# The last eight modulation slabs of a two-block transformer kernel move into the output half of x's first feed-forward

## The chip, the cores and the metric

The kernel runs on one core of a Trainium2 chip. The metric is the time of one execution on the device in microseconds (us), and the median over several runs is what is compared. The five engines of the core are called as in the profile: PE (TensorE), DVE (VectorE), ACT (ScalarE), POOL (GpSimd) and SP (SyncE, which here only issues transfers).

## The reference

Two blocks run one after the other on 256 tokens of width 1024. The first block is attention with a token selection, a short convolution and a layer of 16384 one-neuron experts, of which each token picks 128. The second block takes the first one's output x and a context of 256 tokens. Each block's norms, gates and shifts are modulated by columns that come out of one matrix product with a condition vector:

```python
mod_x = (jax.nn.silu(c) @ w_ada[l] + b_ada[l])[:, None, :]
mod_c = (jax.nn.silu(c_ctx) @ w_ada[l] + b_ada[l])[None, None, :]
sh1x, sc1x, g1x, sh2x, sc2x, g2x, sh3x, sc3x, g3x = jnp.split(mod_x, N_MOD, axis=-1)

x = x + 0.5 * g1x * swiglu(modulate(rmsnorm(x, norm_ffn1[l]), sh1x, sc1x), w13_ffn1[l], w2_ffn1[l])
ctx = ctx + 0.5 * g1c * swiglu(modulate(rmsnorm(ctx, norm_ffn1[l]), sh1c, sc1c), w13_ffn1[l], w2_ffn1[l])
qc, kc, vc, gc, fc, gac, gfc = project(modulate(rmsnorm(ctx, norm_mix[l]), sh2c, sc2c), w_in[l])
...
x = x + g2x * y_x
x = x + 0.5 * g3x * swiglu(modulate(rmsnorm(x, norm_ffn2[l]), sh3x, sc3x), w13_ffn2[l], w2_ffn2[l])
return rmsnorm(x, norm_final)
```

The second block's w_ada is 1024 by 9216: 18 slabs of 512 columns. The first ten hold shift 1, scale 1, gate 1, shift 2 and scale 2; the last eight hold gate 2, shift 3, scale 3 and gate 3, which are wanted only for x, from the mixer's residual on. The context needs nothing of them.

## The kernel before

All weights stream from device memory through one buffer, `ring`, in slabs of 128 partitions by 4096 words (2048 KB; the slabs of a feed-forward's output matrix w2 have 2816 words, 1408 KB). SP issues the slabs in one fixed list (`slab_order`), each as soon as PE has released the slab that held its slot. Up to the experts and the context the ring has four slots. From x's first feed-forward on (`second_at`) it has three (`SPLIT_RING`), and the fourth holds the rounded copies described below.

A modulation slab is used in `mod_steps`. Slab m gives a row group on PE (eight matmuls of the condition columns with the slab), ACT copies the row to `mod_row`, PE turns it into columns (four matmuls of two columns, in `mod_turn`), and ACT copies these to `mod1` or `mod2`. The turn of slab m-1 stands behind the row group of slab m; the last one of a list has its own turn at the end. There are 30 slabs: 0 to 11 for the first block, 12 to 29 for the second.

The program in order of time, as far as it matters here:

- The head: the first block's projections, attention and out projection, with modulation slabs 0 to 14 between them; then the expert queries; then `mod_steps(15, 30)`, fifteen slabs with nothing between them. Beside that, DVE chooses the experts of the first 128 tokens (`choose_experts(0)`).
- The expert loop: 128 batches of two gathered rows each. POOL issues a gather of 1024 KB (128 rows of 8 KB) into one of eight buffers, DVE takes a dot product with it (L1587), ACT applies gelu, DVE scales and sums (L1598), PE sums the other row of the batch. Before its first dot product DVE waits for the last modulation slab: `v.wait_ge(*emptied("mod29"))`. The context's feed-forward and projections are dealt out in pieces between the batches, at fixed batch numbers.
- x's first feed-forward, tag `f1`: eleven slabs of w13, then eight slabs of w2, whose results are called `f1_y0` to `f1_y7`. These products are done in three matmuls of rounded parts. So each slab is cut into pieces (four, or three for w2); ACT writes the upper part of a piece (L924), DVE the rest (L1231), and PE waits for the piece. Four pieces can be ahead.
- The norm `x2`, then the projections `gf`, `f` and so on to the end.

What ACT does during `f1_y` is written out in `norm_hi`: for k from 0 to 7 it calls `ahead("f1_y<k>")`, waits until DVE has added the result to x, and squares block k of x. `ahead(name)` makes an engine first split every piece up to three behind the last piece of `name`. DVE calls the same `ahead` ahead of each of its additions (`take`, L1333). Both engines run their instructions strictly in the order written.

```python
def ahead(name):
    q = piece_of[name]
    split_until(min(q + PIECES, phase_end(q)) - 1)
```

Of the kernel before, what the change touches and what calls it, by code (L numbers as in the profile page):

```python
# [14 lines left out]
P = 128  # L15
# [23 lines left out]
KF = FF // P  # L39
FG = 4  # L40
MODS = [("w_ada", i) for i in range(12)] + [("w_ada_2", i) for i in range(18)]
RING = 4
SLAB = 4096
SPLIT_RING = 3
# [63 lines left out]
def slab_order():  # L108

    mods = [(name, i, SLAB) for name, i in MODS]  # L110
    ffn = lambda n: [(f"w13_ffn{n}", i, SLAB) for i in range(11)] + [(f"w2_ffn{n}", i, KF * P) for i in range(8)]
    w_in_2 = {"q": (0, 2), "k": (2, 4), "v": (4, 8), "g": (8, 12), "f": (12, 14), "ga": (14, 16), "gf": (16, 18)}
    proj = lambda n: [("w_in_2", i, SLAB) for i in range(*w_in_2[n])]
    w_in = lambda i: [("w_in", i, SLAB)]
    out_proj = [("w_out", i, SLAB) for i in range(2)]
    peer = lambda i: [("peer_wq", i, SLAB)]
    first = (mods[:4] + w_in(0) + [("w_idx", 0, KD * 136)] + w_in(1) + w_in(2) + w_in(4) + w_in(5) + w_in(6) + w_in(3)
             + mods[4:13] + out_proj + mods[13:15] + peer(0) + peer(1) + peer(2) + peer(3) + mods[15:])
    context = ffn(1) + proj("k") + proj("v")
    second = (ffn(1) + proj("gf") + proj("f") + [("p_four", i, SLAB) for i in range(2)] + proj("ga") + proj("q")  # L120
              + proj("k") + proj("v") + proj("g") + [("p_ret", i, SLAB) for i in range(4)]
              + [("w_out_2", i, SLAB) for i in range(2)] + ffn(2))
    return first + context + second, len(first) + len(context)
# [33 lines left out]
def program(nc, dram, out):  # L157
# [2 lines left out]

    slabs, second_at = slab_order()
    slots, last_in_split = slots_of(slabs, second_at)
    split = [n for n in range(len(slabs)) if n >= second_at or slabs[n][0] in ("w_in", "w_out", "peer_wq")]
    pieces = [(n,) + cut for n in split for cut in cuts(*slabs[n][:2])]
    first_out = sum(slabs[p[0]][0] == "w_in" for p in pieces)
    first_pieces = sum(p[0] < second_at for p in pieces)
    with ExitStack() as ctx:
        def sb(name, width, dt=F32):
            return ctx.enter_context(nc.sbuf_tensor(name, [P, width], dt))
# [33 lines left out]
        found = sb("found", 2 * PH * PSEL, U32)  # L203
        place = sb("place", SLOTS, U32)
        spare = sb("spare", 2 * PSEL, U32)

        def param(name):
            at, w = PARAM_AT[name]
            return prm[:, at:at + w]
# [42 lines left out]
        probs = [arena[:, G0 + 7936:G0 + 8960].rearrange("p (h s) -> p h s", h=HEADS),  # L252
                 arena[:, F0 + 3072:F0 + 5120].rearrange("p (h s) -> p h s", h=HEADS)]
        subkeys = arena[:, G0 + 9984:G0 + 12032].rearrange("p (h n) -> p h n", h=2 * PH)
        mod_row = small[:, 1536:2560].rearrange("p (a n) -> p a n", a=2)
        y_att = arena[:, F0 + 5120:F0 + 6144].rearrange("p (j t) -> p j t", j=KA)

        pq_t = arena[:, G0:G0 + 4096].rearrange("p (h t) -> p h t", h=2 * PH)
# [106 lines left out]
        def _(pe):  # L365
# [29 lines left out]
            def mm(o, a, b, first, last):  # L395
                return nc.tensor.matmul(o, a, b, start=first, stop=last)  # L396
# [11 lines left out]
            def mod_turn(m):  # L408

                pe.wait_ge(*emptied(f"row{m}"))  # L410
                o = begin(f"mod{m}", "act")
                a, w = (0, 1) if MODS[m][0] == "w_ada" else (1, 2)
                for j in range(4):
                    last = mm(o[:, j * w:(j + 1) * w], mod_row[:, m % 2, j * P:(j + 1) * P], const("pick3")[:, a:a + w], True, True)
                end(last)
                turned[0] += 1

# [90 lines left out]
            def split_feed_forward(tag, m, f):  # L508
                need = norm_need(m)
                for i in range(11):  # L510
                    for half, who in ((0, "act"), (1, "dve")):
                        name = f"{tag}_{'ab'[half]}{i}"
                        o = begin(name, who)
                        for j in range(2):
                            _, w_hi, w_lo = next_piece()
                            for k in range(KD):
                                if k in need:
                                    pe.wait_ge(*need.pop(k))
                                last = three(o[:, j * L:(j + 1) * L], w_hi[:, k, :], w_lo[:, k, :], h_hi[:, k, :],
                                             h_lo[:, k, :], k == 0, k == KD - 1)  # L520
                            piece_end(last, name if j else None)
                for i in range(8):
                    o = begin(f"{tag}_y{i}", "dve")
                    for part in range(3):
                        (k0, k1, _, _), w_hi, w_lo = next_piece()
                        if i == 0:

                            pe.wait_ge(sem("hid_split"), 11 * f + k1 // 2)
                        for k in range(k0, k1):
                            last = three(o[:, 0:L], w_hi[:, k - k0, :], w_lo[:, k - k0, :], hid_hi[:, k, :],  # L530
                                         hid_lo[:, k, :], k == 0, k == KF - 1)
                        piece_end(last, f"{tag}_y{i}" if part == 2 else None)

            def squares_by_block(tag, sq=sq2):
                o = begin("ss_" + tag, "dve")
# [105 lines left out]
            for t in range(NT):  # L641
                for i in range(2):
# [1 line left out]
                    for j in range(4):  # L644
                        last = nc.tensor.transpose(o[:, j * P:(j + 1) * P], h_t[:, 4 * i + j, t * P:(t + 1) * P], ident)
                    end(last)
            mod_steps(15, 30)
            at = [0]

            def ctx_end(name, ins):  # L650
# [251 lines left out]
        def _(act):  # L902
# [58 lines left out]
            def mod_row_of(m):  # L961
                if m >= 2:

                    act.wait_ge(group_done, index[f"mod{m - 2}"] + 1)
                copy_out(f"row{m}", mod_row[:, m % 2, :])

            def mod_turned(m):
                turned[0] += 1
# [15 lines left out]
            def norm_hi(tag, m, shift, names, sq=sq2, hi=h_hi):  # L984

                for k in range(KD):
                    if names:
                        name = names[k * len(names) // KD]
                        ahead(name)
                        act.wait_ge(*emptied(name))  # L990
                    nc.scalar.activation(sq[:, k, :], x_t[:, k, :], ACT.Square).then_inc(sem("sq_" + tag), 1)
                root(rstd[:])
                if m is not None:
                    normed_hi(m, shift, hi)
# [94 lines left out]
            for t in range(NT):  # L1089
                for i in range(2):  # L1090
                    copy_out(f"ht{t}_{i}", h2[:, t, i * BANK:(i + 1) * BANK])
            mod_steps(15, 30)

            def context():

# [117 lines left out]
        def _(v):  # L1213
# [331 lines left out]
            def context():  # L1545
# [1 line left out]
                yield 0  # L1547
                step(TT(mod1[:, 40:48], mod1[:, 40:48], param("b_ada")[:, 40:48], ALU.add))
                m2 = mod2[:].rearrange("p (j s) -> p j s", s=2)
                step(TT(m2, m2, param("b_ada_2").unsqueeze(2).to_broadcast([P, 72, 2]), ALU.add))  # L1550
                for key, row, s in (("ctx1", 2, 1), ("x1", 2, 0), ("x3", 8, 0)):
                    step(TS(half_gate[key], mod2_v[:, row, :, s], 0.5, None, ALU.mult))
                yield done_at["ss_ctx1"] + 1
                v.wait_ge(sem("ctx_landed"), 16)
# [21 lines left out]
            v.wait_ge(*emptied("ks1_3"))  # L1576
            v.sem_inc(sem("row_free_pe"), GBUF // 2)
            v.sem_inc(sem("row_free_dve"), GBUF // 2 + 1)
            v.wait_ge(*emptied("mod29"))

            def dot_batch(n):

# [63 lines left out]
            v.wait_ge(sem("late"), 64)  # L1646
            split_ff_dve("f1", 0, half_gate["x1"])
            split_modulated("x2", 3, param("norm_mix_2"), mod2_v[:, 4, :, 0], mod2_v[:, 3, :, 0])
            ahead("f3")
            for i in range(4):  # L1650
                o = take(f"mx{i}")
# [166 lines left out]
```

## Time and profile before

| | |
|---|---|
| three runs, median (lowest to highest) | 2064.69 us (2057.81 to 2064.85) |
| the profiled execution, its own time | 2061.91 us |
| its span in the trace | 2060.1 us |
| granted PE clock, mean of the span | 0.915 of full |
| PE busy | 1746.9 us, 85% |
| DVE busy | 1265.4 us, 61% |
| ACT busy | 601.0 us, 29% |
| POOL busy | 433.6 us, 21% |
| moved from device memory | 535.86 MB, 261 GB/s over the span |

Busy shares are means over stages with different limits. The trace gives for each instruction its start from the span's beginning, its length, the idle time of its engine before it and what ended that idle time. For a transfer it gives the time from issue to landing. The profiled execution's own time exceeds its span by 1.8 us, which lies outside of the program.

### The profile page before, as it was taken

The numbers are of one execution on the slowest core, as the hardware profiler recorded it, in microseconds if no ns is written. First come the engines' busy times: TensorE is split into PE (matmuls) and PEld (weight loads), VectorE is DVE, ScalarE is ACT, GpSimd is POOL, SyncE is SP. The second block draws the span as 40 slices with busy tenths as digits, with TensorE's granted clock in tenths as the row PEclk, the third lists the DMA queues.
The fourth block names the chain that finished last, engine by engine and source line by source line (L and its number), as shares of the span: only waits on it lengthen the run. The fifth ranks groups of instructions, "written<-read, shape, count | busy, mean of one in ns | idle before, by whom it ended". The sixth has DMA issues, their size and how long they took to land.

```text
span 2060.1 us, 25356 instructions
## 1 busy us (share of the span) xinstructions
PE 1746.9 (85%) x9904; PEld 1349.1 (65%) x9904; DVE 1265.4 (61%) x2226; ACT 601.0 (29%) x899; POOL 433.6 (21%) x344
## 2 busy tenths in 40 slices
PE   5996898668787877866689669999999999999997
PEld 2984794335554545543333227999879996689997
DVE  2674366288788786766867575564525645665554
ACT  3434342211111110000000016754434443245442
POOL 1550461033333334333334310000000000000000
PEclk7998798689998998888899779999999999999999
DMA  7446638989999999999899961445425452153542
GB/s 327 154 186 273 262 128 376 426 359 387 397 353 381 367 389 379 387 406 387 350 411 403 403 248 69 178 166 189 158 82 202 170 202 82 47 199 130 198 147 100
DMA packets 57570, 538.51 MB, mean 261 GB/s; under 512 B 6384, under 2 KB 6512, under 8 KB 7152
## 3 DMA queue, kind: packets, MB, share of 16 engines
q1 hardware_dynamic: 20592, 268.48, 33.4%
q0 software_dynamic: 36864, 268.45, 32.7%
q8 instruction: 78, 1.28, 0.3%
q14 instruction: 36, 0.29, 0.0%
HBM read 535.86 MB, written 1.05 MB: 261 GB/s over the span
## 4 chain that ended last, share of the span: by engine, by line
PE 60%; DMA 22%; DVE 8%; issue 6%; POOL 2%; ACT 1%; POOLq 0%; DVEq 0%; another core or an unknown queue 0%; SPq 0%; ACTq 0%
PE psum L396 60%; DMA arena<-in_experts,idx_stage 17%; DMA ring<-in_w_ada 3%; POOL arena L895 1%; DVE arena L1598 1%; DMA ring<-in_w_in 1%; DVE rstd L1258 1%; DVE small L1597 1%; DVE small L1595 0%; DVE arena L1587 0%; DVE h_t L1292 0%; ACT upper L924 0%; DVE small L1587 0%; DVE h_t L1272 0%; DVE h_t L1270 0%
## 5 line engine op out<-in xcount | busy, mean ns | idle before, releaser
L396 PE MATMUL psum<-arena,small 128*128 128x512 f32 x560 | 322.2, 708 | 204.2 <-DVE small L1597 204.0
L1587 DVE CUSTOM_DVE_ANT_0 arena<-arena 128x1024 f32<-128x1024 f32 x256 | 313.7, 1225 | 239.3 <-DMA arena<-in_experts,idx_stage 179.4
L1231 DVE TENSOR_TENSOR ring_r<-ring,ring_r 128x1024 fp32r<-128x1024 f32 (+1 forms) x240 | 287.7, 1207 | 277.1 <-ACT ring_r L924 276.0
L396 PE MATMUL psum<-small_r,ring_r 128*128 128x256 f32 x2304 | 417.0, 281 | 9.4 <-DVE h_t_r L1298 9.4
L895 POOL DMA_INDIRECT arena<-in_experts,idx_stage x256 | 297.5, 1162 | 410.1 <-PE psum L396 333.8
L396 PEld LDWEIGHTS psum<-small_r,ring_r 128*128 128x128 f32 x2304 | 361.8, 189 | 11.2 <-issue 10.5
L396 PEld LDWEIGHTS psum<-arena,small 128*128 128x128 f32 x560 | 114.3, 216 | 356.2 <-DVE small L1597 250.6
L396 PE MATMUL psum<-h_t_r,ring_r 128*128 128x256 f32 x1152 | 329.9, 286 | 0.0
L396 PE MATMUL psum<-arena_r,ring_r 128*128 128x256 f32 x2208 | 326.3, 281 | 2.8 <-DVE arena_r L1280 2.8
L924 ACT ACTIVATE ring_r<-ring 128x1024 fp32r<-128x1024 f32 (+1 forms) x240 | 248.7, 1042 | 217.0 <-PE psum L396 213.8
L396 PEld LDWEIGHTS psum<-arena_r,ring_r 128*128 128x128 f32 x2208 | 290.6, 189 | 3.3 <-DVE arena_r L1280 3.2
L1133 ACT ACTIVATE small<-small 128x2 f32<-128x2 f32 x128 | 26.0, 203 | 704.6 <-DVE small L1587 704.5
L396 PEld LDWEIGHTS psum<-h_t_r,ring_r 128*128 128x128 f32 x1152 | 218.5, 190 | 0.1
L396 PEld LDWEIGHTS psum<-h_t,ring 128*128 128x128 f32 x720 | 141.6, 197 | 43.1 <-issue 25.5
L396 PE MATMUL psum<-h_t,ring 128*128 128x256 f32 x720 | 167.6, 387 | 0.0
L1598 DVE SCALAR_TENSOR_TENSOR arena<-arena,small 128x1024 f32<-128x1024 f32 x128 | 163.7, 1279 | 0.0
L873 POOL TENSOR_TENSOR ring_r<-ring,upper 128x1024 fp32r<-128x1024 f32 x52 | 125.4, 2432 | 180.6 <-ACT upper L924 180.6
L396 PE MATMUL psum<-arena_r,upper 128*128 128x256 f32 x768 | 143.7, 290 | 4.7 <-DVE arena_r L1298 4.7
L396 PEld LDWEIGHTS psum<-arena_r,upper 128*128 128x128 f32 x768 | 122.1, 196 | 6.4 <-issue 5.6
L396 PE MATMUL psum<-ring,cols 128*32 128x512 f32 x480 | 76.9, 778 | 34.9 <-DMA ring<-in_w_ada 30.3
L396 PE MATMUL psum<-ring,h_t 128*128 128x512 f32 (+1 forms) x224 | 91.9, 553 | 0.0
L396 PE MATMUL psum<-arena 128*128 128x128 f32 (+4 forms) x368 | 85.2, 408 | 4.9 <-ACT arena L947 3.4
(210 smaller groups left out, 1509.2 us busy)
## 6 DMA issues: line engine op xcount, KB each, us to landing
ring<-in_w_ffn SPq DMA_DIRECT2D x33, 2048.0 KB, 7.8
ring<-in_w_in SPq DMA_DIRECT2D x31, 2048.0 KB, 7.5
ring<-in_w_ada SPq DMA_DIRECT2D x30, 2048.0 KB, 10.7
ring<-in_w_ffn SPq DMA_DIRECT2D x24, 1408.0 KB, 6.3
ring<-in_w_out SPq DMA_DIRECT2D x4, 2048.0 KB, 8.1
ring<-in_peer_wq SPq DMA_DIRECT2D x4, 2048.0 KB, 7.4
ring<-in_p_ret SPq DMA_DIRECT2D x4, 2048.0 KB, 7.6
arena<-in_experts,idx_stage POOLq DMA_INDIRECT x256, 10.2
```

Source lines behind the costliest of these rows:

```text
L396: return nc.tensor.matmul(o, a, b, start=first, stop=last)
L873: nc.gpsimd.tensor_tensor(whole(i, ring_r), whole(i, ring), upper(i).bitcast(F32), ALU.subtract).then_inc(lo_made, 1)
L895: nc.gpsimd.indirect_dma_start(rows[slot % GBUF], None, dram["experts"], bass.IndirectOffsetOnAxis(ap=idx_stage[:, slot:slot + 1], axis=0) ...
L924: nc.scalar.activation(upper(i), whole(i, ring), ACT.Copy).then_inc(hi_made, 1)
L1133: nc.scalar.activation(acts[:, n % 8, :], dots[:, n % 8, :], ACT.Gelu_apprx_tanh).then_inc(sem("gelus"), 1)
L1231: nc.vector.tensor_tensor(whole(i, ring_r), whole(i, ring), upper(i).bitcast(F32), ALU.subtract).then_inc(lo_made, 1)
L1258: step(nc.vector.reciprocal(dst, dst), sem("root_in"))
L1587: step(nc.vector.tensor_tensor_reduce(u, u, h2[:, n // PER_TILE, :], 1.0, 0.0, ALU.mult, ALU.add, dots[:, n % 8, s:s + 1]), sem("dots"))
L1597: TS(diag[:, n % (GBUF // 2), :], ident, weights[:, n % 8, 0:1], None, ALU.mult).then_inc(sem("diag"), 1)
L1598: STT(y_of[t], rows[(BATCH * n + 1) % GBUF][:, D:2 * D], weights[:, n % 8, 1:2], y_of[t], ALU.mult, ALU.add).then_inc(sem("row_free_dve"), 1)
```

## The change

Modulation slabs 22 to 29 leave the head. In the slab list they now stand between the w2 slabs of x's first feed-forward: slabs 22 to 26 behind w2 slabs 0 to 4, one each, and slabs 27, 28 and 29 behind w2 slab 7. PE and ACT do their share of each at the same places: PE behind the matmuls of `f1_y<k>`, ACT behind the square of block k. DVE no longer waits for `mod29` but for `mod21` ahead of the expert loop, adds the bias to 80 columns of mod2 there instead of 144, and does the rest, with the halved gate 3, behind the norm `x2`. The row copies of the moved slabs go to two other places in the memory. The moved slabs are not cut into pieces.

```diff
+LATE_MODS = 22
+MOD_CTX = LATE_MODS - 12
+
+def late_mods(k):
+    return (LATE_MODS + k, LATE_MODS + k + 1) if k < 5 else (LATE_MODS + 5, len(MODS)) if k == KD - 1 else (0, 0)
...
-             + mods[4:13] + out_proj + mods[13:15] + peer(0) + peer(1) + peer(2) + peer(3) + mods[15:])
+             + mods[4:13] + out_proj + mods[13:15] + peer(0) + peer(1) + peer(2) + peer(3) + mods[15:LATE_MODS])
     context = ffn(1) + proj("k") + proj("v")
-    second = (ffn(1) + proj("gf") + proj("f") + [("p_four", i, SLAB) for i in range(2)] + proj("ga") + proj("q")
+    ffn_x = ffn(1)[:11]
+    for k, slab in enumerate(ffn(1)[11:]):
+        ffn_x += [slab] + mods[slice(*late_mods(k))]
+    second = (ffn_x + proj("gf") + proj("f") + [("p_four", i, SLAB) for i in range(2)] + proj("ga") + proj("q")
...
                         piece_end(last, f"{tag}_y{i}" if part == 2 else None)
+                    if f == 0:
+                        mod_steps(*late_mods(i), i == KD - 1)
...
-            mod_steps(15, 30)
+            mod_steps(15, LATE_MODS)
...
                     nc.scalar.activation(sq[:, k, :], x_t[:, k, :], ACT.Square).then_inc(sem("sq_" + tag), 1)
+                    if tag == "x2":
+                        mod_steps(*late_mods(k), k == KD - 1)
...
-                for key, row, s in (("ctx1", 2, 1), ("x1", 2, 0), ("x3", 8, 0)):
+                for key, row, s in (("ctx1", 2, 1), ("x1", 2, 0)):
...
-            v.wait_ge(*emptied("mod29"))
+            v.wait_ge(*emptied(f"mod{LATE_MODS - 1}"))
...
             split_modulated("x2", 3, param("norm_mix_2"), mod2_v[:, 4, :, 0], mod2_v[:, 3, :, 0])
+            v.wait_ge(*emptied(f"mod{len(MODS) - 1}"))
+            late_cols = mod2[:].rearrange("p (j s) -> p j s", s=2)[:, 4 * MOD_CTX:72, 0]
+            step(TT(late_cols, late_cols, param("b_ada_2")[:, 4 * MOD_CTX:72], ALU.add))
+            step(TS(half_gate["x3"], mod2_v[:, 8, :, 0], 0.5, None, ALU.mult))
```

SP's list of transfers in x's first feed-forward, before: eight w2 slabs (128x2816) in a row, and the projections' slabs (`in_w_in`, the first four of them `gf` and `f`) behind them.

```order
L850 DMA ring<-in_w_ffn 128x4096 x8
L850 DMA ring<-in_w_ffn 128x2816 x8
L850 DMA ring<-in_w_in 128x4096 x4
L850 DMA ring<-in_p_four 128x4096 x2
L850 DMA ring<-in_w_in 128x4096 x14
```

The same place of SP's list now, from w2 slab 3 on:

```order
L866 DMA ring<-in_w_ffn 128x2816
L866 DMA ring<-in_w_ada 128x4096
L866 DMA ring<-in_w_ffn 128x2816
L866 DMA ring<-in_w_ada 128x4096
L866 DMA ring<-in_w_ffn 128x2816 x3
L866 DMA ring<-in_w_ada 128x4096 x3
L866 DMA ring<-in_w_in 128x4096 x4
```

With three slots, a slab is issued when the slab three places ahead of it is released: modulation slab 29 at the release of w2 slab 7, and the first `gf` slab (first of `in_w_in`) at the release of modulation slab 27, where before it was issued at the release of w2 slab 5.

ACT at the end of `f1_y` before: the splits of the first `gf` slab (`ring_r<-ring 128x1024 x3`), the square of block 7, the root of the norm.

```order
L924 ACTIVATE ring_r<-ring 128x1024 x2
L924 ACTIVATE ring_r<-ring 128x768
L991 ACTIVATE small<-x_t 128x256
L924 ACTIVATE ring_r<-ring 128x1024 x3
L991 ACTIVATE small<-x_t 128x256
L909 ACT_TABLE_LOAD
L909 ACTIVATE rstd<-rstd 128x256
```

ACT at the same place now; the 128x512 copies out of psum are the rows of slabs 27, 28 and 29, the 128x8 copies the turned columns of 26 to 29:

```order
L940 ACTIVATE ring_r<-ring 128x1024 x2
L940 ACTIVATE ring_r<-ring 128x768
L1007 ACTIVATE small<-x_t 128x256
L940 ACTIVATE ring_r<-ring 128x1024 x3
L1007 ACTIVATE small<-x_t 128x256
L963 ACTIVATE arena<-psum 128x512
L963 ACTIVATE mod<-psum 128x8
L963 ACTIVATE small<-psum 128x512
L963 ACTIVATE mod<-psum 128x8
L963 ACTIVATE arena<-psum 128x512
L963 ACTIVATE mod<-psum 128x8 x2
L925 ACT_TABLE_LOAD
```

Six copies (seven instructions) come between the last square and the root, and all of them stand behind the three splits of the `gf` slab.

PE at the end of `f1_y` before: 528 matmuls of the w2 slabs, the eight matmuls that sum the squares (`small,ones`), then the `gf` projection.

```order
L396 MATMUL psum<-arena_r,ring_r 128x256 x528
L396 MATMUL psum<-small,ones 128x256 x8
L396 MATMUL psum<-small_r,ring_r 128x256
L396 MATMUL psum<-h_t_r,ring_r 128x256
```

PE now, from the last modulation slab that stands alone; `ring,cols` is a row group, `early,small` and `early,arena` are turns:

```order
L410 MATMUL psum<-ring,cols 32x512 x8
L410 MATMUL psum<-early,arena 128x2 x4
L410 MATMUL psum<-arena_r,ring_r 128x256 x198
L410 MATMUL psum<-ring,cols 32x512 x8
L410 MATMUL psum<-early,small 128x2 x4
L410 MATMUL psum<-ring,cols 32x512 x8
L410 MATMUL psum<-early,arena 128x2 x4
L410 MATMUL psum<-ring,cols 32x512 x8
L410 MATMUL psum<-early,small 128x2 x4
L410 MATMUL psum<-early,arena 128x2 x4
L410 MATMUL psum<-small,ones 128x256 x8
```

The 528 matmuls are now in parts of 66 with a row group and mostly a turn between them, and three row groups and four turns stand between the last 198 and the sum of the squares.

## Rows read from the trace of the kernel before

**Rows 1.** The page, 40 slices: busy tenths of DMA, and GB/s

```profile
DMA  7446638989999999999899961445425452153542
GB/s 327 154 186 273 262 128 376 426 359 387 397 353 381 367 389 379 387 406 387 350 411 403 403 248 69 178 166 189 158 82 202 170 202 82 47 199 130 198 147 100
```

**Rows 2.** The chain that ended last: start us, us, what it was

```profile
342.01 19.87 DMA ring<-in_w_ada
...
365.29 26.11 DMA ring<-in_w_ada
...
1225.71 225.33 PE psum L396 x1680
```

**Rows 3.** Timeline of PE, the head's last modulation slabs: start us, us

```profile
339.56 2.42 PE L396 MATMUL psum<-ring,cols 128*32 128x512 f32 x16 [1.16 <-DMA ring<-in_w_ada]
...
349.35 1.92 PE L396 MATMUL psum<-ring,cols 128*32 128x512 f32 x16 [0.41 <-DMA ring<-in_w_ada]
351.20 1.05 PE L396 MATMUL psum<-early,small 128*128 128x2 f32 x8
...
391.44 3.64 PE L396 MATMUL psum<-ring,cols 128*32 128x512 f32 x16 [1.93 <-DMA ring<-in_w_ada]
395.01 2.15 PE L396 MATMUL psum<-early,small 128*128 128x2 f32 x16
```

**Rows 4.** Timeline of DVE around the start of the expert loop

```profile
397.41 1.23 DVE L1587 CUSTOM_DVE_ANT_0 arena<-arena 128x1024 f32<-128x1024 f32 x1 [54.85 <-ACT mod L947]
...
414.31 1.22 DVE L1587 CUSTOM_DVE_ANT_0 arena<-arena 128x1024 f32<-128x1024 f32 x1 [1.40 <-DMA arena<-in_experts,idx_stage]
```

**Rows 5.** Timeline of POOL: the first and the eighth gather

```profile
349.19 1.12 POOL L895 DMA_INDIRECT arena<-in_experts,idx_stage  x1 [6.01 <-issue]
...
358.09 0.94 POOL L895 DMA_INDIRECT arena<-in_experts,idx_stage  x1 [0.30 <-issue]
```

**Rows 6.** DMA issues of these two: count, median us from issue to landing

```profile
arena<-in_experts,idx_stage POOLq DMA_INDIRECT x1, 13.3
...
arena<-in_experts,idx_stage POOLq DMA_INDIRECT x1, 56.1
```

**Rows 7.** Windows: busy us of each engine, PE clock, DMA share, GB/s

```profile
370.00:380.00 10.00, 8.06 (x40) 2.77 (x32) 0.00 (x0) 0.78 (x2) 0.00 (x0) 0.50 1.00 423
430.00:435.00 5.00, 3.78 (x4) 1.18 (x4) 4.79 (x12) 0.41 (x2) 0.00 (x0) 0.50 0.24 98
440.00:445.00 5.00, 4.37 (x17) 2.78 (x16) 4.09 (x7) 0.20 (x1) 2.13 (x3) 1.00 1.00 401
```

**Rows 8.** Timeline of PE, sum of squares x1, then the end of f1

```profile
1225.71 6.66 PE L396 MATMUL psum<-small,ones 128*128 128x256 f32 x16 [3.44 <-ACT small L991]
...
1385.22 62.35 PE L396 MATMUL psum<-arena_r,ring_r 128*128 128x256 f32 x528
1447.40 3.62 PE L396 MATMUL psum<-small,ones 128*128 128x256 f32 x16
1455.71 0.55 PE L396 MATMUL psum<-small_r,ring_r 128*128 128x256 f32 x1 [4.70 <-DVE h_t_r L1298]
```

**Rows 9.** DMA issues at 1384 to 1386 and 1447 to 1448 us

```profile
ring<-in_w_ffn SPq DMA_DIRECT2D x1, 1408.0 KB, 6.1
...
ring<-in_w_in SPq DMA_DIRECT2D x1, 2048.0 KB, 7.5
```

**Rows 10.** Timeline of ACT: a row copy in the head, then the end of f1

```profile
395.21 0.60 ACT L947 ACTIVATE small<-psum 128x512 f32<-128x512 f32 x1 [5.49 <-PE psum L396]
...
1445.48 1.06 ACT L924 ACTIVATE ring_r<-ring 128x1024 fp32r<-128x1024 f32 x1 [1.77 <-PE psum L396]
1448.22 0.42 ACT L991 ACTIVATE small<-x_t 128x256 f32<-128x256 f32 x1 [1.69 <-DVE x_t L1333]
```

**Rows 11.** Timeline of DVE at the end of f1

```profile
1446.57 1.22 DVE L1231 TENSOR_TENSOR ring_r<-ring,ring_r 128x1024 fp32r<-128x1024 f32 x1 [1.60 <-ACT ring_r L924]
1447.72 0.48 DVE L1333 SCALAR_TENSOR_TENSOR x_t<-psum,cols,x_t 128x256 f32<-128x256 f32 x1
```

More of the change, by code:

```diff
@@ L162, in program @@
     slots, last_in_split = slots_of(slabs, second_at)
-    split = [n for n in range(len(slabs)) if n >= second_at or slabs[n][0] in ("w_in", "w_out", "peer_wq")]
+    split = [n for n in range(len(slabs)) if (n >= second_at and slabs[n][0] != "w_ada_2") or slabs[n][0] in ("w_in", "w_out", "peer_wq")]
     pieces = [(n,) + cut for n in split for cut in cuts(*slabs[n][:2])]
@@ L205, in program, with mod_row @@
         spare = sb("spare", 2 * PSEL, U32)
+        def mod_row(m):
+            return (early_row if m < LATE_MODS else late_row)[m % 2]
         def param(name):
@@ L254, in program @@
         subkeys = arena[:, G0 + 9984:G0 + 12032].rearrange("p (h n) -> p h n", h=2 * PH)
-        mod_row = small[:, 1536:2560].rearrange("p (a n) -> p a n", a=2)
+        early_row = [small[:, 1536:2048], small[:, 2048:2560]]
+        late_row = [small[:, 2048:2560], arena[:, G0 + 7680:G0 + 8192]]
         y_att = arena[:, F0 + 5120:F0 + 6144].rearrange("p (j t) -> p j t", j=KA)
@@ L413, in mod_turn @@
                 for j in range(4):
-                    last = mm(o[:, j * w:(j + 1) * w], mod_row[:, m % 2, j * P:(j + 1) * P], const("pick3")[:, a:a + w], True, True)
+                    last = mm(o[:, j * w:(j + 1) * w], mod_row(m)[:, j * P:(j + 1) * P], const("pick3")[:, a:a + w], True, True)
                 end(last)
@@ L964, in mod_row_of @@
                     act.wait_ge(group_done, index[f"mod{m - 2}"] + 1)
-                copy_out(f"row{m}", mod_row[:, m % 2, :])
+                copy_out(f"row{m}", mod_row(m))
             def mod_turned(m):
@@ L1091, in _ @@
                     copy_out(f"ht{t}_{i}", h2[:, t, i * BANK:(i + 1) * BANK])
-            mod_steps(15, 30)
+            mod_steps(15, LATE_MODS)
             def context():
@@ L1549, in context @@
                 m2 = mod2[:].rearrange("p (j s) -> p j s", s=2)
-                step(TT(m2, m2, param("b_ada_2").unsqueeze(2).to_broadcast([P, 72, 2]), ALU.add))
-                for key, row, s in (("ctx1", 2, 1), ("x1", 2, 0), ("x3", 8, 0)):
+                m2 = m2[:, 0:4 * MOD_CTX, :]
+                step(TT(m2, m2, param("b_ada_2")[:, 0:4 * MOD_CTX].unsqueeze(2).to_broadcast([P, 4 * MOD_CTX, 2]), ALU.add))
+                for key, row, s in (("ctx1", 2, 1), ("x1", 2, 0)):
                     step(TS(half_gate[key], mod2_v[:, row, :, s], 0.5, None, ALU.mult))
```

## The prediction

> **What bounds the kernel now.** I read the page first, for where the DMA engines are full: from slice 7 to slice 24 of 40, at 51.5 us each from 309 to 1236 us, they stand at 8 or 9 tenths, and at 6 or less later on [rows 1]. That stretch holds the last modulation slabs of the head and the expert loop. Then the chain that ended last, in order of time: it names modulation slabs as what ended the waits at 342.01 (19.87 us long) and at 365.29 (26.11 us), the gathers after that, and from 1225.71 on PE, for 225.33 us without a break, which is all of x's first feed-forward [rows 2]. So the change takes work out of a stage that waits for transfers and puts it into a stage in which PE is the bound.
>
> In the head, PE's timeline shows the last slabs: the row group of slab 29 starts at 391.44, and the two last turns end at 397.16 [rows 3]. DVE then starts the expert loop at 397.41, after 54.85 us of idleness that ACT's copy of the last columns ended [rows 4]: it was done with choosing experts at 342.56. The row group of slab 21 starts at 339.56 and lasts 2.42 us [rows 3]; with its own turn behind it (2.15 us for two) slab 21 is finished at about 344.4.
>
> **The head: what is gained.** The wait for slab 29 becomes one for slab 21, 53 us earlier. DVE can't use all of it: the first gather is issued at 349.19 and takes 13.3 us to land, at 362.5; the eighth is issued at 358.09 and takes 56.1, to 414.2 [rows 5, 6]. So seven gathers land in 51.7 us, 7.4 us each. Before, only the eighth was waited for: DVE idled 1.40 us for it and went on at 414.31 [rows 4]. Each is 1.05 MB, and the engines moved 423 GB/s in that time at a share of 1.00 [rows 7], so gathers got 142 GB/s, a third; slabs got the rest.
>
> After the change SP has only four slabs to issue at this place, those of the context's feed-forward, in the place of slabs 22 to 25; the last of them is issued at 342.01 and lands at 361.9 [rows 2]. The next slab waits until PE has used the first of the four, which the loop does later. From 362 on gathers have the engines alone. A stretch of the loop with full engines moves 401 GB/s [rows 7]: 1.05 MB takes 2.6 us. The eighth gather lands at 362.5 + 7 x 2.6 = 380.7 instead of 414.2, and DVE is **33.5 us** earlier at its dot product. Bounds: at 423 GB/s 2.5 us each, 34.5; DVE itself needs from its first dot product to the eighth 414.31 - 397.41 - 1.40 = 15.5 us, so 378.0 at the earliest, which allows 35 and no more. At 387 GB/s, a usual slice of the loop [rows 1], it is 2.7 us each and 32.1.
>
> Does the loop keep it? Its batches, the context's pieces and the slabs have fixed places relative to each other, so all shifts alike. The eight slabs' 16.8 MB are 39.7 us at 423 GB/s, more than 33.5; the other 6 don't come back, because the engines were not full anyway a little later: 0.24 from 430 to 435 [rows 7]. There DVE works on the context's norm and no buffer comes free.
>
> The Trainium skill, "DMA: Bandwidth & Descriptors", section "Issuing engines are not separate DMA queues", says that transfers of all issuing engines run on the same 16 DMA engines and interleave. By that rule alone every byte taken out of a full stretch comes back, 39.7 us and not 33.5. The trace agrees with the sharing (142 of 423 GB/s above), but its 0.24 says that the stretch ends too soon for all of it.
>
> **Inside f1_y: what is paid.** PE needs for the eight w2 slabs 62.35 us without a break [rows 8], 7.8 each. At full clock a row group takes 1.85 us to the start of what follows, a turn 1.05 [rows 3]. Behind w2 slabs 0 to 4 there are five row groups and four turns: 5 x 1.85 + 4 x 1.05 = 13.4 us. Nothing hides them, PE is the chain.
>
> Do slabs still come in time? A w2 slab takes 6.1 us to land, one of 2048 KB 7.5 [rows 9], and behind another still moving only its own bytes: 1.44 MB / 423 = 3.4 us, 2.1 MB / 423 = 5.0. Counting from the start of w2 slab 0: slab 23 is issued at 7.8 and lands at 15.3; w2 slab 2 is issued at the release of slab 22, at 9.6, lands at 18.7, and is cut by ACT (1.06) and DVE (1.22, [rows 10, 11]), ready at 21.1. PE is ready for it after w2 slab 1, row group 23 and turn 22 at 9.6 + 7.8 + 1.85 + 1.05 = 20.3. One stall of 0.8 us. For the following ones the same count has PE and slab meet within half a microsecond, and PE late. Sum of this part: **14.2 us**; bounds 13.4 and 13.4 + 4 x 0.8 = 16.6.
>
> **Behind f1_y7: the wait.** Let E be the end of w2 slab 7 on PE. Before, E is the start of the squares' sum at 1447.40, and the `gf` matmuls start at 1455.71, E + 8.3 [rows 8]. `gf`'s first slab had long landed. Now:
> - Slab 29 is issued at E and lands at E + 7.5. The first `gf` slab is issued at the release of slab 27, E + 1.9, behind it in the queue: E + 12.5.
> - ACT stands in `ahead("f1_y7")` and waits for that slab, though it has nothing to do with slabs 27 to 29. Behind that instruction are queued the square of block 7 and all six copies. DVE stands there too, its addition of `f1_y7` behind the splits; PE, after row group 28, waits at turn 27 for ACT's copy of row 27.
> - From landing on: ACT's first split 1.06, DVE's three at 1.22 each, its addition 0.48, the square 0.42, the row copy 0.60 [rows 10, 11]: 1.06 + 3.66 + 0.48 + 0.42 + 0.60 = 6.2. PE resumes at E + 18.7.
> - PE has then idled some 14 us. After such gaps the rows of the head show granted 0.50, the 1.2 GHz level [rows 7], and there a row group with the two turns behind it takes 397.16 - 391.44 = 5.7 us [rows 3]. With turn 27 (1.05 to 2.1, I take 1.9): E + 26.3. At the 2.4 GHz level it would be 5.0 in all, E + 23.7.
> - The squares' sum takes 3.62 at the full clock and 6.66 at half after a gap [rows 8]. By then PE has worked for 7.6 us, so I take 3.6: E + 29.9. From its end to the `gf` matmuls 1455.71 - 1451.02 = 4.7 as before: **E + 34.6**.
>
> That is 26.3 us more than E + 8.3; bounds 23.7 (clock full throughout) and 29.4 (squares at half too). Of the 26.3 some 10 are PE's work on slabs 27 to 29, and 16 are waiting.
>
> "TensorE: Matmul & The Clock Gate" of the Trainium skill, section "HAM oscillation — how this bites in real kernels", describes this pattern: bursts of matmuls shorter than the waits between them each start at half clock. By it the end of this stretch would be at half throughout, E + 37.7, and the sum 3 us higher.
>
> The bias of the last 32 columns and gate 3 are two small DVE instructions behind the norm, under 0.5 us beside PE's work on pieces already cut; two as small go from the head. I count both at nothing; uncovered they cost 0.5.
>
> **The sum.** -33.5 + 14.2 + 26.3 = +7.0, between -35 + 13.4 + 23.7 = +2.1 and -32.1 + 16.6 + 29.4 = +13.9. Against the profiled execution's own 2061.91 that is 2068.9. The median of the three runs lies 2.8 above that execution, so a median after may lie as far above; I take **2070 us**.
>
> **The rivals.**
> - *The order costs nothing but work* (faster). If ACT's wait for the `gf` slab were hidden, the moved work would cost 13.4 and three row groups and four turns, 3 x 1.85 + 4 x 1.05 = 9.8: -33.5 + 23.2 = -10.3, 2052 us. It decides by when the `gf` slab lands: it must be cut at E, 12.5 us earlier than I count. Against it: SP issues in order, with three slots. For it: only that the trace of before has no case of such a wait. Chance 0.1.
> - *Bytes are the bound of the loop*, the whole 39.7 us come back: +0.8, 2063. For it: the loop's slices stand at 9 tenths throughout [rows 1]; against it the 0.24. Chance 0.15.
> - *The clock falls in f1 too*. In the head the granted clock was 0.50 over 10 us of which PE was busy with row groups and turns for 8.06 [rows 7]. If each of the five insertions costs the half clock over the row group, the turn and some 2 us of the next slab: 5 x (2.9 + 1) = 19 us more, 2088; with half of them 2079. Against it: PE has no gap there. Chance 0.2, both sizes together.
> - *Gathers stay at 7.4 us each* although they are alone, because their own queue limits them: nothing is gained in the head, +40, 2102. Against it: in the loop 401 GB/s flow with hardly a slab among them. Chance 0.05.
>
> **How the numbers follow.** My forecast has 0.5, its own range is 2064 to 2076. The range reaches to the first rival's 2052 and short of the half-clock case in full: 2053 to 2083; outside are the last rival, part of the third and part of the first. A measurement of this kernel can tell about 0.5% from no change, here 2054.4 and 2075.0. Faster: the first rival, and a trace of the second, 0.12. Slower: the last rival, the third, and the upper tail of the forecast, 0.32. Within: 0.56.
>
> **What would show it.** Right, if DVE's first dot product starts at about 362.5 and the eighth at about 381; if in f1 PE has eight parts of 7.8 us at clock 1.00; if ACT idles for some 10 us until the slab of `in_w_in` lands, and PE for some 14 us between row group 28 and turn 27; if `gf` starts 7 us later than 1455.71. Wrong, if the eighth gather lands near 414, if the loop's length (from the eighth dot product to the squares at 1225.71) changes by over 3 us, or if PE goes from w2 slab 7 to `gf` in under 20 us.

## The result, and the profile after

| | median | lowest to highest | runs |
|---|---|---|---|
| after | 2072.68 us | 2068.95 to 2079.71 | 6 |
| before, beside it | 2063.95 us | 2057.81 to 2066.94 | 6 |

The ratio is 1.0049, interval 1.0027 to 1.0071. A second measurement (r_after_again, below) gave 1.0048, 1.0030 to 1.0065. So the change costs 9 to 10 us (8.7 by the medians, 10.1 by the ratio), just under the 0.5% named in the prediction but outside of the noise of both measurements, and the forecast of 2070 us holds. The profiled execution took 2068.95 us with a span of 2067.1: 7.0 more span than before.

The page of the kernel after, DMA and GB/s, to be held against [rows 1]:

```profile
DMA  7456639899899999998999715477324552153542
GB/s 326 164 193 264 255 126 427 325 399 369 366 381 372 374 398 379 398 402 341 405 386 386 309 48 198 169 279 305 123 82 173 195 188 97 42 193 135 202 145 100
```

The slice from 362 to 413 us fell from 426 to 325 GB/s, and the two slices from 1343 on, which hold `f1_y` after the change, rose from 166 and 189 to 279 and 305.

**The head.** DVE's first and eighth dot product (the line is L1606 now), POOL's first and eighth gather, and the chain's piece for the eighth:

```profile
355.63 1.23 DVE L1606 CUSTOM_DVE_ANT_0 arena<-arena 128x1024 f32<-128x1024 f32 x1 [18.60 <-DMA arena<-in_experts,idx_stage]
...
373.59 1.23 DVE L1606 CUSTOM_DVE_ANT_0 arena<-arena 128x1024 f32<-128x1024 f32 x1 [0.54 <-DMA arena<-in_experts,idx_stage]
```

```profile
343.65 1.12 POOL L911 DMA_INDIRECT arena<-in_experts,idx_stage  x1 [6.00 <-issue]
...
352.55 0.94 POOL L911 DMA_INDIRECT arena<-in_experts,idx_stage  x1 [0.30 <-issue]
```

```profile
352.55 20.90 DMA arena<-in_experts,idx_stage
373.45 0.03 issue
```

DVE no longer waits for a slab but for gathers. The eighth takes 20.90 us to land where it took 56.1 [rows 6]. The first took 11.8 us and landed at 355.45, so from the first landing to the eighth it is 373.45 - 355.45 = 18.0 us for seven gathers, 2.57 us each, against 7.4 before. The whole execution was 5.5 us early already where the row group of slab 15 starts (318.02 before, 312.49 after), so the stage is counted from there: to the eighth dot product 96.3 us before, 61.1 after.

**x's first feed-forward, output half.** PE, to be held against the one row of 62.35 us in [rows 8]:

```profile
1350.89 7.94 PE L410 MATMUL psum<-arena_r,ring_r 128*128 128x256 f32 x66
1358.76 1.92 PE L410 MATMUL psum<-ring,cols 128*32 128x512 f32 x16
...
1370.44 1.05 PE L410 MATMUL psum<-early,small 128*128 128x2 f32 x8
1372.32 8.01 PE L410 MATMUL psum<-arena_r,ring_r 128*128 128x256 f32 x66 [0.83 <-DVE ring_r L1249]
...
1395.10 9.54 PE L410 MATMUL psum<-arena_r,ring_r 128*128 128x256 f32 x66 [1.20 <-DVE ring_r L1249]
...
1407.34 23.57 PE L410 MATMUL psum<-arena_r,ring_r 128*128 128x256 f32 x198
1430.83 1.93 PE L410 MATMUL psum<-ring,cols 128*32 128x512 f32 x16
1432.69 1.05 PE L410 MATMUL psum<-early,small 128*128 128x2 f32 x8
1433.67 1.92 PE L410 MATMUL psum<-ring,cols 128*32 128x512 f32 x16
1449.41 1.87 PE L410 MATMUL psum<-early,arena 128*128 128x2 f32 x8 [13.82 <-ACT arena L963]
1451.21 3.51 PE L410 MATMUL psum<-ring,cols 128*32 128x512 f32 x16
1454.65 1.05 PE L410 MATMUL psum<-early,small 128*128 128x2 f32 x8
1455.56 1.03 PE L410 MATMUL psum<-early,arena 128*128 128x2 f32 x8
1456.45 3.70 PE L410 MATMUL psum<-small,ones 128*128 128x256 f32 x16
1464.85 0.55 PE L410 MATMUL psum<-small_r,ring_r 128*128 128x256 f32 x1 [4.69 <-DVE h_t_r L1316]
```

The w2 slabs took 1430.83 - 1350.89 = 79.9 us instead of 62.2. In the part of 9.54 us PE was busy throughout, but the granted clock fell, shortly behind the wait of 1.20 us (a window: busy us of PE, PEld, DVE, ACT, POOL, then clock, DMA share, GB/s):

```profile
1397.00:1399.00 2.00, 2.00 (x11) 2.00 (x11) 0.35 (x1) 0.97 (x3) 0.00 (x0) 0.50 1.00 427
```

0.50 is the 1.2 GHz level. From 1400 on the clock was 1.00 again, the 2.4 GHz level.

From the end of w2 slab 7 (E = 1430.83) to `gf` it is 34.0 us instead of 8.3, with an idle time of 13.82 in the middle that ACT's row copy ended. What ACT waited for stands in its own timeline, and the last line is SP's part of the chain, the first `gf` slab:

```profile
1423.69 0.42 ACT L1007 ACTIVATE small<-x_t 128x256 f32<-128x256 f32 x1 [1.79 <-DVE x_t L1351]
1443.38 2.95 ACT L940 ACTIVATE ring_r<-ring 128x1024 fp32r<-128x1024 f32 x3 [19.27 <-DMA ring<-in_w_in]
1448.46 0.42 ACT L1007 ACTIVATE small<-x_t 128x256 f32<-128x256 f32 x1 [2.13 <-DVE x_t L1351]
1448.78 0.58 ACT L963 ACTIVATE arena<-psum 128x512 f32<-128x512 f32 x1
```

```profile
1432.82 10.47 DMA ring<-in_w_in
```

ACT stood from 1424.11 to 1443.38 before a split that PE needed only after the norm. Row 27 had been ready to copy since 1432.8 and was copied at 1448.78.

### The profile page after: what moved, and what is told of

The parts are those of the page before. It is cut to its first block, busy times and chain, and to the rows that moved or that the text cites. A ratio compares the mean times of both kernels' runs of the same rounds, so it can differ in the third digit from the quotient of the medians.

```text
span 2067.1 us, 25358 instructions
## 1 busy us (share of the span) xinstructions
PE 1731.6 (84%) x9904; PEld 1341.3 (65%) x9904; DVE 1263.9 (61%) x2227; ACT 598.8 (29%) x899; POOL 440.5 (21%) x344
## 3 DMA queue, kind: packets, MB, share of 16 engines
HBM read 535.86 MB, written 1.05 MB: 260 GB/s over the span
## 4 chain that ended last, share of the span: by engine, by line
PE 58%; DMA 20%; DVE 12%; issue 6%; POOL 2%; ACT 1%; POOLq 0%; DVEq 0%; SPq 0%; ACTq 0%
PE psum L410 58%; DMA arena<-in_experts,idx_stage 17%; POOL arena L911 2%; DMA ring<-in_w_in 1%; DMA ring<-in_w_ffn 1%; DVE arena L1617 1%; DVE rstd L1276 1%; DVE small L1616 1%; DVE arena L1489 0%; DVE small L1536 0%; DVE h_t L1310 0%; DVE small L1487 0%; DMA ring<-in_w_ada 0%; DVE small L1490 0%; DVE arena L1535 0%
## 5 line engine op out<-in xcount | busy, mean ns | idle before, releaser
L1606 DVE CUSTOM_DVE_ANT_0 arena<-arena 128x1024 f32<-128x1024 f32 x256 | 313.8, 1226 | 209.6 <-DMA arena<-in_experts,idx_stage 204.8
L410 PEld LDWEIGHTS psum<-h_t,ring 128*128 128x128 f32 x720 | 141.1, 196 | 43.3 <-issue 25.7
L963 ACT ACTIVATE arena<-psum 128x512 f32<-128x512 f32 (+2 forms) x109 | 59.1, 556 | 114.7 <-PE psum L410 109.1
## 6 DMA issues: line engine op xcount, KB each, us to landing
arena<-in_experts,idx_stage POOLq DMA_INDIRECT x256, 10.1
```

What stands on the lines that cost most here:

```text
L963: drain(nc.scalar.activation(dst, take(name)[:, 0:width], func, scale=scale))
L1606: step(nc.vector.tensor_tensor_reduce(u, u, h2[:, n // PER_TILE, :], 1.0, 0.0, ALU.mult, ALU.add, dots[:, n % 8, s:s + 1]), sem("dots"))
```

## The experiments

All stages below are read from the profiled execution of each kernel. "Head" runs from the row group of slab 15 to the eighth dot product, "loop" from there to the squares of x1, "w13" over the input half of f1, "w2" from the first w2 matmul to `gf`. In the last two columns stand the difference of head, w13 and w2 to the kernel before, and the timed difference (ratio less 1, times the median before) with its interval. The stages leave out the time ahead of slab 15's row group (312.2 to 321.0 us), the 32.2 to 33.8 us between the squares of x1 and w13, and what follows `gf` (602.2 to 605.0).

```
kernel          head   loop    w13     w2     stages  timed
before          96.3   811.4  125.8   70.5
r_before_1      96.3   821.2  125.8   70.5
r_before_2      96.3   817.8  125.8   70.5
after           61.1   819.1  124.6  114.0    +7.1   +10.1 (5.6 to 14.7)
r_after         60.8   819.2  125.8  116.7   +10.7
r_after_again   60.9   826.0  125.8  111.6    +5.7    +9.9 (6.2 to 13.4)
e_left_out      60.8   826.5  125.8   70.5   -35.5   -37.7 (-43.7 to -31.8)
e_wait_only     95.7   821.7  125.8   70.5    -0.6    +3.5 (-0.8 to +8.0)
e_split_late    61.1   822.2  125.8  104.8    -0.9    -1.4 (-5.6 to +2.9)
e_one_each      62.4   827.1  125.8  106.5    +2.1    +1.4 (-2.3 to +5.0)
e_each_split    60.9   819.5  125.8  100.3    -5.6    -5.6 (-8.7 to -2.5)
e_w13           61.0   811.4  152.4   70.5    -8.7    -4.1 (-8.5 to 0.0)
e_w13_again     60.7   823.5  152.2   70.5    -9.2    -8.3 (-11.8 to -4.5)
```

**The same kernels again.** Nothing edited; these give the spread of the stages.

> The changed kernel once more, for a second trace. Both theories expect the same in x's first feed-forward: some 80 us from the first w2 slab to the end of the eighth, some 34 from there to gf. If the 6.4 us by which the expert loop was longer in the first trace after (977.3 us from the eighth dot product to the first w2 slab, 970.9 before) come from the change, the loop has 977 again; if a loop of 128 batches waiting for transfers simply varies, it has some other number between 965 and 985.

> The kernel before once more, for a second trace. If the loop of batches simply varies, its length from the eighth dot product to the sum of squares x1 is not again 811.4 us but anything between 805 and 830; if the change makes the loop longer (819 to 827 in four of five traces with it), it is again 811 to 813.

> The kernel before a third time, for the same question: loop 811 to 813 if the change is what makes it longer, otherwise somewhere between 805 and 830.

> The changed kernel once more, timed beside the other two. By stages of the traces: 35.3 us less in the head, 43.5 to 46.2 more from the first w2 slab to gf, so 8 to 11 us more than before, 1.004 to 1.005. Were the loop of batches longer by the 3 us that separates the means of the traces so far, it would be 1.006.

They took 2077.19, 2066.59, 2062.89 (one execution each) and 2076.14 us (median of 6). r_after had 977.2 us from the eighth dot product to the first w2 slab, the very 977 that its expectation took as a sign that the change made the loop longer. But the kernel before, once more, had 980.7 and 977.3 there (r_before_1 and r_before_2), so that number says nothing of the change. The head is the same within 0.3 us for one kernel, but the loop runs from 811.4 to 821.2 us in three executions of the kernel before, and from 819.1 to 826.0 after. A difference of some us in the loop between two traces is therefore nothing that the change did. The end of w2 differs too. In r_after PE stayed at half clock after the same idle time:

```profile
1451.32 1.87 PE L410 MATMUL psum<-early,arena 128*128 128x2 f32 x8 [13.72 <-ACT arena L963]
1453.12 3.64 PE L410 MATMUL psum<-ring,cols 128*32 128x512 f32 x16
1456.69 1.87 PE L410 MATMUL psum<-early,small 128*128 128x2 f32 x8
1458.42 1.84 PE L410 MATMUL psum<-early,arena 128*128 128x2 f32 x8
1460.13 6.53 PE L410 MATMUL psum<-small,ones 128*128 128x256 f32 x16
```

The squares took 6.53 us there and 3.70 above, the turns 1.87 and 1.05. The granted clock was 0.50 from 1451.3 to 1460.1, where the execution above had 1.00 from 1454.6 on. That is 4.5 us between two executions of one kernel, E to `gf` 38.5 and 34.0 us.

**Without the late slabs (e_left_out).** Is the gain of the head kept to the end? This kernel leaves out slabs 22 to 29 with all their work; their columns are zeros.

```diff
-MODS = [("w_ada", i) for i in range(12)] + [("w_ada_2", i) for i in range(18)]
+MODS = [("w_ada", i) for i in range(12)] + [("w_ada_2", i) for i in range(10)]
...
-    return (LATE_MODS + k, LATE_MODS + k + 1) if k < 5 else (LATE_MODS + 5, len(MODS)) if k == KD - 1 else (0, 0)
+    return (0, 0)
```

> The changed kernel with modulation slabs 22 to 29 left out of the computation (their columns are set to zero), so that gate 2, shift 3, scale 3 and gate 3 come from the bias alone: the head's gain without the price. Theory: head and loop together give 33.5 us less than before, x's first feed-forward is as before (70.5 us from the first w2 slab to gf): 0.984 of before. Rival (every byte comes back): 39.7 less, 0.981. Second rival (the head's gain is lost again in the loop): 10 to 25 less.

Measured 2028.00 us against 2062.08. The timed difference holds the stage's -35.5 in its interval, and w2 is back at 70.5 without the slabs. So the head's gain reaches the end. The interval also allows 39.7 (all the bytes). The head stage gave 35.5; whether the loop gave some us more this kernel can't tell, because its one trace, with a loop of 826.5, is of the slowest of its seven executions (2041.41 us, 13 above the median).

**The wait alone (e_wait_only).** In the kernel before, only DVE's wait is moved to slab 21; slabs 22 to 29 stay where they were, and what DVE does with the last columns goes behind the norm `x2`, as in the change.

```diff
-            v.wait_ge(*emptied("mod29"))
+            v.wait_ge(*emptied("mod21"))
```

> The kernel before with DVE's wait alone changed: it waits for slab 21 instead of 29, all slabs stay in the head, the bias of the late columns goes behind the norm x2. Theory (slabs and gathers share the DMA engines, and PE works on slabs in order): the eighth gather still lands near 414 and PE gets to the first batch only behind slab 29, so the first dot product is 35 us earlier but the eighth and the whole are not: within 3 us of before, 0.999 to 1.001. Rival (the wait itself was the cost): 20 to 33 us less.

Measured 2066.92 us against 2062.08, ratio 1.0017 (0.9996 to 1.0039). DVE's dot products are the first, second and eighth:

```profile
356.73 1.23 DVE L1588 CUSTOM_DVE_ANT_0 arena<-arena 128x1024 f32<-128x1024 f32 x1 [19.55 <-DMA arena<-in_experts,idx_stage]
364.10 1.23 DVE L1588 CUSTOM_DVE_ANT_0 arena<-arena 128x1024 f32<-128x1024 f32 x1 [6.14 <-DMA arena<-in_experts,idx_stage]
...
408.39 1.23 DVE L1588 CUSTOM_DVE_ANT_0 arena<-arena 128x1024 f32<-128x1024 f32 x1 [2.47 <-DMA arena<-in_experts,idx_stage]
```

Counted from slab 15, the first comes within 1 us of where it is after the change (44.1 us behind it, 43.1 after), the eighth only 0.6 us earlier than before. So the wait alone gives nothing; the gain of the head needs the 16.8 MB to leave it. Here 426 GB/s were moved from 358 to 395 us, and seven gathers landed in 51.7 us, 7.4 each as before, a third of that.

**The `gf` splits behind the copies (e_split_late).** ACT and DVE split the first `gf` slab behind slab 29's copies and behind the addition of `f1_y7`, instead of ahead.

```diff
-                        ahead(name)
+                        if name != "f1_y7":
+                            ahead(name)
...
+                if tag == "x2":
+                    ahead("f1_y7")
```

> Only the order on ACT and DVE changes: the three splits of the first gf slab stand behind the modulation copies instead of ahead of block 7's addition and square. My theory (the copies are queued behind a wait for a slab they don't need): from the end of the eighth w2 slab (E) row groups and turns run on, wait for slab 29 at E + 7.5, and gf starts at about E + 21 instead of E + 34: 13 us less than the change, about 2060 us, 0.998 of before. Rival (the time is that of slab 29's and gf's transfers and of the half clock, the order doesn't matter): gf can't start before its slab is there and cut, at E + 12.5 + 3 to 5, and the norm's chain behind it; within 3 us of the change, 2070 to 2073.

Measured 2064.42 us against 2066.30. w2 fell from 114.1 (mean of three) to 104.8. PE, from slab 27 on:

```profile
1434.78 1.92 PE L410 MATMUL psum<-ring,cols 128*32 128x512 f32 x16
...
1443.04 2.61 PE L410 MATMUL psum<-ring,cols 128*32 128x512 f32 x16 [2.51 <-DMA ring<-in_w_ada]
1445.58 1.87 PE L410 MATMUL psum<-early,small 128*128 128x2 f32 x8
1447.31 1.84 PE L410 MATMUL psum<-early,arena 128*128 128x2 f32 x8
1449.02 6.34 PE L410 MATMUL psum<-small,ones 128*128 128x256 f32 x16
```

The 13.8 us of waiting have become 2.51, now for slab 29 itself. E to `gf` is 1460.05 - 1434.78 = 25.3 us instead of 33.7 to 38.5, where E + 21 was expected. Half clock over the squares ate 2.6 of what was won, and over the two turns ahead of them 1.6. This shows that the order on ACT and DVE was the cause of the long wait: nothing else differs.

**One slab behind each w2 slab (e_one_each).** Slabs 27 and 28 go behind w2 slabs 5 and 6, so that `gf`'s first slab is issued 2 places earlier.

```diff
-    return (LATE_MODS + k, LATE_MODS + k + 1) if k < 5 else (LATE_MODS + 5, len(MODS)) if k == KD - 1 else (0, 0)
+    return (LATE_MODS + k, LATE_MODS + k + 1)
```

> One modulation slab behind each of the eight w2 slabs instead of three behind the last. Theory: what costs is the pile behind the last w2 slab. With slabs 27 and 28 earlier, the w2 part gets 5.5 us longer (85.4 instead of 79.9), but gf's first slab lands at E + 1.7, and gf starts at about E + 17.5 instead of E + 34: 11 us less than the change, 2060 to 2064 us. Rival (the cost is the ring with three slots: any big slab among the w2 slabs stalls PE, wherever it stands): three more stalls of 1 to 2 us, and nothing gained behind the last, 2072 to 2076.

Measured 2067.51 us against 2066.30, w2 106.5:

```profile
1445.77 1.92 PE L410 MATMUL psum<-ring,cols 128*32 128x512 f32 x16
1447.62 1.05 PE L410 MATMUL psum<-early,small 128*128 128x2 f32 x8
1453.59 1.87 PE L410 MATMUL psum<-early,arena 128*128 128x2 f32 x8 [4.91 <-ACT arena L963]
1455.31 6.71 PE L410 MATMUL psum<-small,ones 128*128 128x256 f32 x16
```

The wait behind the splits is still there, 4.91 us, and after it the squares ran at half clock, 6.71 instead of 3.70. The squares were as slow behind this gap of 5 us as in r_after behind one of 14. E to `gf` is 21.0 us, where 17.5 was expected.

**Both (e_each_split).** The edits of the last two together.

> Both remedies together: one modulation slab behind each w2 slab, and the splits of gf's first slab behind the last modulation copies. Theory: the two costs were apart, the pile of three and the wait in ACT's order. From the first w2 slab to gf 97.7 us (106.45 with one each alone, less the 4.9 us that PE waited for ACT, less some 4 us of half clock behind that gap); before had 70.5 and the change 114.0 to 116.7. So 16 to 19 us less than the change, 0.996 to 0.997 of before. Rival (with one slab each the last modulation slab's landing takes over as what is late): 103 to 106 us for that stretch and 1.000 of before.

Measured 2061.48 us against 2066.42, ratio 0.9973 (0.9958 to 0.9988); w2 100.3:

```profile
1444.05 1.93 PE L410 MATMUL psum<-ring,cols 128*32 128x512 f32 x16
1445.91 1.05 PE L410 MATMUL psum<-early,small 128*128 128x2 f32 x8
1446.82 1.03 PE L410 MATMUL psum<-early,arena 128*128 128x2 f32 x8
1447.71 3.70 PE L410 MATMUL psum<-small,ones 128*128 128x256 f32 x16
1457.31 0.55 PE L410 MATMUL psum<-small_r,ring_r 128*128 128x256 f32 x1 [5.89 <-DVE h_t_r L1319]
```

No gap is left behind the last w2 slab, and the clock stays. E to `gf` is 13.3 us. The norm's tail grew from 4.69 to 5.89, because the `gf` splits now stand between the sum and the root on ACT and DVE. w2 is 29.8 us longer than before. Of these 23.3 are the eight row groups and turns, 1.2 the norm's tail, 3.1 three waits for pieces of 0.81, 1.30 and 0.97 us, and 1.5 a w2 part of 9.54 us again, with the clock at 0.54 from 1401.3 to 1405.0; 0.7 stay open. So the forecast of 97.7 us was 2.6 short.

**In the input half (e_w13).** The eight slabs go behind w13 slabs 0 to 7 instead, one each; `ahead` and the copies are dealt out the same way there.

```diff
-    ffn_x = ffn(1)[:11]
-    for k, slab in enumerate(ffn(1)[11:]):
+    ffn_x = []
+    for k, slab in enumerate(ffn(1)):
...
+                    if f == 0 and i < 9:
+                        mod_late(i)
```

> The eight slabs stand behind w13 slabs 0 to 7 instead of behind w2 slabs; ACT splits ahead before it copies a row. A w13 slab takes PE 11.4 us, so the slab behind it (at most 12.5 us for two in a row) has time. Theory: only PE's own work is left, 8 x (1.85 + 1.05) = 23.2 us where the change pays 43.4 (17.7 in the w2 part, 25.7 behind it): 20 us less than the change, 2052 to 2054 us, 0.995 of before. Rival (every modulation slab costs a stall of 1 to 2 us in a ring of three slots, or the clock falls): 2060 to 2068.

> The version with the slabs behind w13 slabs 0 to 7 once more, to narrow its interval beside the change on the same chip. The trace had 26.6 us more in the w13 part, nothing in the w2 part and behind it. Theory: less than before by 35.3 - 26.6 = 8.7 us, 0.996; 17 to 20 us less than the change. Rival (what the first series said, 0.998): 4 us less than before.

Measured 2060.34 us against 2066.30 (ratio 0.998, 0.9959 to 1.0) and 2059.69 against 2066.42 (0.996, 0.9943 to 0.9978): the lowest medians of the complete versions, though e_each_split's 0.9973 lies within this interval. The 20 us less than the change that e_w13 was to bring (0.995 of before) came out as 14 to 18. The input half grew by 26.6 and 26.4 us, w2 not at all. Two rows at which PE waited for a piece, in e_w13, and the window of this half in e_w13_again:

```profile
1249.12 0.38 PE L410 MATMUL psum<-small_r,ring_r 128*128 128x256 f32 x1 [1.00 <-DVE ring_r L1260]
...
1278.87 0.38 PE L410 MATMUL psum<-small_r,ring_r 128*128 128x256 f32 x1 [0.78 <-DVE ring_r L1260]
```

```profile
1234.86:1387.09 152.23, 150.35 (x1250) 136.87 (x1250) 75.50 (x77) 88.59 (x108) 0.00 (x0) 1.00 0.61 241
```

The full clock throughout and at most 1 us of waiting at a time: what remains is work, 8 x (1.86 + 1.05) = 23.3 us, and stalls of 1.7 in all in e_w13_again (0.93, 0.56 and 0.24). Some 1.4 us of the 26.4 stand in neither, and what they are stays open.

## Why the prediction was right

**The head, -33.5 us.** It was 35.2 to 35.5 in three traces. A gather took 2.57 us, as counted (2.6), but the first landed 11.8 us after its issue, not 13.3. The three bounds of this term were worked out wrongly: the rows give 414.31 - 378.0 = 36.3 for DVE's own work, not 35, some 34.3 at 423 GB/s, not 34.5, and 32.7 at 387 GB/s, not 32.1. The measured gain lies within these, and with them the sum runs from +0.8 to +13.3 instead of +2.1 to +13.9. The first dot product stands at 355.63 instead of "about 362.5" and the eighth at 373.59 instead of 381; 5.5 us of both are the early start of this execution. That the sharing of the DMA engines, and not the wait, held DVE was the reason given, and e_wait_only shows it from the other side. The Trainium skill, "DMA: Bandwidth & Descriptors", section "Issuing engines are not separate DMA queues", says that transfers of all issuing engines run on the same 16 DMA engines and interleave. The traces agree: beside slabs a gather took 7.4 us, without them 2.57.

**Does the loop keep it?** Yes, by the timed difference of e_left_out. But the sign that I named, a loop changed by over 3 us, would have spoken against me: it went from 811.4 to 819.1 in the first pair. The repeats show that this length scatters by 10 us in the kernel before alone. Over the three traces before it is 816.8 in the mean, over the eight with the same loop and the late slabs 821.0; a real loss of a few us is neither shown nor excluded by the traces, and the timed differences, which mostly agree with the sums without it, leave little room for it. The sign was badly chosen; the head from slab 15 to the eighth dot product is a good one.

**Inside `f1_y`, +14.2 us.** It was +17.7, +15.9 and +15.7, the first over the bound of 16.6. The five row groups and four turns cost 13.2 of it (13.4 counted). The waits for pieces were two instead of one, 0.83 and 1.20 us; the first is the 0.8 that the count had. Behind the second the granted clock was 0.50 from 1397 to 1399, which made that part 1.5 us longer; in r_after, behind a wait of 1.04, it stayed at 1.00:

```profile
1398.64 8.01 PE L410 MATMUL psum<-arena_r,ring_r 128*128 128x256 f32 x66 [1.04 <-DVE ring_r L1249]
```

The other parts took 7.9 to 8.0 us from start to start, and the last three together 23.5, where the count had 7.8 each: 1.0 us in all, in r_after too, which no run explains (in r_after_again the last three took 22.6). A slab of `in_w_ada` issued at 1380.37 took 8.7 us to land and the w2 slab issued 1.9 behind it 10.2, where I had counted 7.5 and 9.1.

**Behind `f1_y7`, +26.3 us.** It was 34.0 - 8.3 = +25.7 in the profiled execution, +25.4 in r_after_again, and +30.2 with the squares at half clock in r_after, over the bound of 29.4. The end at half clock throughout, which the prediction put at E + 37.7, is thus what one of three executions had, at E + 38.5. The mechanism stands in the rows step by step: slab landed at E + 12.5 (1443.3), PE back at E + 18.6 (1449.41), squares at E + 25.6. I had E + 12.5, 18.7 and 26.3. e_split_late took most of the wait away by the order alone.

**The rivals.** *The order costs nothing but work*: no, 13.8 us of waiting; but with the order mended (e_each_split), w2 grows by 29.8, and that version is faster than before, by 5.6 us where this rival had 10.3. *Bytes are the bound*: the head gave 35, and the timed differences speak against 4 us more from the loop: with them the stages of the change would add up to +3.6 in the mean of its three traces, below both of its timed intervals. *The clock falls in f1*: not in the five insertions, whose row groups took 1.92 us each, but once inside the fifth w2 slab, shortly behind a wait of some 1.2 us, in the profiled execution, e_split_late and e_each_split. That cost 1.5 us and not 19; "PE has no gap there" was not so. *Gathers stay at 7.4 us*: 2.57.

Stages of one kernel add up to +5.7 to +10.7 over three traces, and timed it is +10. The forecast of +7.0 was low by what `f1_y` cost beyond the count and by the squares' half clock in some executions, and the head's extra 1.7 us made up for a part. The mechanism of each term is in the rows; that the errors of the terms have opposite signs is luck. Of the signs named, `gf` started 9.1 us later instead of 7, and the eight parts were not all at 7.8 us and clock 1.00.

## What to carry to other kernels

When work moves from a stage bound by transfers to one bound by its engine, the moved work is paid in full, so it must be less than the bytes gained; here 23 us of PE work against 35 us of head left 12 at best, 9 by the stages of the best version (4 to 8 timed), and in the change some 20 us of waits and half clock ate more than that. Look at each engine's queue for an instruction that prefetches for the next stage and stands ahead of copies that this stage needs: once its transfer is put behind others, everything behind it waits. And put such work one slab at a time where transfers have slack and no norm or other short serial part follows.

## What was not expected of the hardware

- The same instructions don't take the same time from execution to execution where gathers set the pace: the loop took 811.4 to 821.2 us in three executions of the kernel before and 811.4 to 827.1 in the eight with the late slabs. The row group of slab 15 started between 312.2 and 321.0 us. The stages bound by PE repeat more closely: w2 without the slabs took 70.5 in all seven traces that have it so, w13 125.8 in ten of eleven and 124.6 in the profiled execution after, for a reason that stays open.
- Whether the granted clock returns within the last 7 us of work after a gap of 14 us differs between executions with the same rows: the squares took 3.70 us in two and 6.53 in one. After 4.91 us of idleness they took 6.71 (one trace), after 2.51 us 6.34 (one trace). The same scatter stands behind far shorter waits: in the fifth w2 slab the clock fell to 0.50 behind waits of 1.16, 1.20 and 1.30 us in three traces, and stayed at 1.00 behind 1.04, 1.24 and 1.42 in three others.
- Beside slabs a gather of 1.05 MB got a third of the bandwidth (7.4 us), without slabs it took 2.57 us.
